# Three tiles ahead on ScalarE, one one-hot instruction for four tokens, and another order of fetches in a fused two-block kernel

## The reference, cut to what matters

```python
def peer_ffn(x, w_q, sub_keys, expert_u, expert_v):
    ...
    vals, ci = lax.top_k(cand, P_TOPK)
    e = (jnp.take_along_axis(i1, ci // P_TOPK, axis=-1) * N_KEYS
         + jnp.take_along_axis(i2, ci % P_TOPK, axis=-1))
    g = jax.nn.softmax(vals, axis=-1)
    ...
        a = jnp.einsum('cd,ckd->ck', xc, expert_u[ec])
        w = (gc * jax.nn.gelu(a.astype(jnp.float32))).astype(x.dtype)
        return jnp.einsum('ck,ckd->cd', w, expert_v[ec])
```

## Time and profile before

| | us |
|---|---|
| median of 3 runs (2543.43 to 2550.14) | 2543.64 |
| the profiled execution's own time | 2543.99 |
| its span, first to last instruction | 2542.3 |

### The profile page before, as it was taken

One profiled execution on the slowest core, in us unless ns is written; L12 is line 12 of the kernel. 1 busy time (PEld: TensorE's weight loads), 2 busy tenths in 40 slices (PEclk: granted clock), 3 DMA queues, 4 the chain that ended last, 5 costly groups with the idle time before them and its releaser, 6 DMA issues.

```text
span 2542.3 us, 39573 instructions
## 1 busy us (share of the span) xinstructions
PE 2397.2 (94%) x14819; PEld 2116.5 (83%) x14819; DVE 1463.5 (58%) x3355; ACT 1115.1 (44%) x1958; POOL 374.0 (15%) x338
## 2 busy tenths in 40 slices
PE   7999999999999888999999998888878999999999
PEld 4888788888785555779999998888877999999999
DVE  4444444333654485441899998777758773444443
ACT  4444343222442376343433448877853332332322
POOL 0000000000200000100001002222334313433330
PEclk9999999999998799998999999999998999999999
DMA  4223222322430000121556658887899988999992
GB/s 151 99 74 100 90 97 77 100 88 87 163 107 21 1 1 1 50 100 67 160 160 188 203 167 290 292 282 274 286 335 357 340 285 327 347 362 332 357 352 102
DMA packets 131823, 462.11 MB, mean 182 GB/s; under 512 B 13840, under 2 KB 32528, under 8 KB 129888
## 3 DMA queue, kind: packets, MB, share of 16 engines
q1 hardware_dynamic: 75744, 233.87, 26.9%
q0 software_dynamic: 51440, 196.90, 21.5%
q10 hardware_dynamic: 4496, 29.36, 3.0%
HBM read 407.12 MB, written 52.43 MB: 181 GB/s over the span
## 4 chain that ended last, share of the span: by engine, by line
PE 77%; DVE 12%; ACT 8%; DMA 1%; issue 1%; POOL 0%; ACTq 0%; SPq 0%; DVEq 0%; POOLq 0%
PE bank L427 13%; PE bank L428 13%; PE bank L429 13%; PE bank L1092 7%; PE bank L1093 7%; PE bank L1094 7%; DVE wlo L414 3%; PE bank L1105 2%; ACT stage L1478 2%; PE bank L442 2%; ACT hot L1464 1%; PE bank L1060 1%; PE bank L524 1%; ACT hot L1459 1%; ACT whi L410 1%; PE bank L707 1%
## 5 line engine op out<-in xcount | busy, mean ns | idle before, releaser
L414 DVE TENSOR_TENSOR wlo<-raw,whi 128x1024 fp32r<-128x1024 f32 x398 | 485.5, 1225 | 540.0 <-ACT whi L410 482.3
L427 PE MATMUL bank<-act_hi,whi 128*128 128x384 f32 (+1 forms) x1968 | 730.4, 371 | 31.9 <-DVE wlo L414 18.4
L428 PE MATMUL bank<-act_lo,whi 128*128 128x384 f32 (+1 forms) x1968 | 718.8, 365 | 0.0
L429 PE MATMUL bank<-act_hi,wlo 128*128 128x384 f32 (+1 forms) x1968 | 718.0, 365 | 0.0
L410 ACT ACTIVATE whi<-raw 128x1024 fp32r<-128x1024 f32 x398 | 418.3, 1056 | 288.2 <-PE bank L1094 175.2
L427 PEld LDWEIGHTS bank<-act_hi,whi 128*128 128x128 f32 x1968 | 375.8, 191 | 81.5 <-DVE wlo L414 21.0
L429 PEld LDWEIGHTS bank<-act_hi,wlo 128*128 128x128 f32 x1968 | 375.5, 191 | 38.1
L428 PEld LDWEIGHTS bank<-act_lo,whi 128*128 128x128 f32 x1968 | 376.0, 191 | 35.7 <-issue 0.5
L1092 PE MATMUL bank<-h_hi,whi 128*128 128x384 f32 x1024 | 350.2, 342 | 6.5 <-DVE h_lo L2196 6.5
L1093 PE MATMUL bank<-h_lo,whi 128*128 128x384 f32 x1024 | 348.0, 340 | 0.0
L1094 PE MATMUL bank<-h_hi,wlo 128*128 128x384 f32 x1024 | 345.8, 338 | 0.0
(11 more groups left out here) (354 smaller groups left out, 2765.5 us busy)
## 6 DMA issues: line engine op xcount, KB each, us to landing
raw<-tiles SPq DMA_DIRECT2D x398, 512.0 KB
acts_dram<-gelu SPq DMA_DIRECT2D x128, 192.0 KB
gates_dram<-stage ACTq DMA_DIRECT2D x12, 2048.0 KB
wg<-gates_dram POOLq DMA_DIRECT2D x16, 1536.0 KB
hf<-acts_dram POOLq DMA_DIRECT2D x16, 1536.0 KB
bias<-alibi POOLq DMA_DIRECT2D x16, 256.0 KB, 3.0
w1s<-cmp_w POOLq DMA_DIRECT2D x1, 4096.0 KB, 13.8
res<-x_t ACTq DMA_DIRECT2D x4, 512.0 KB, 10.0
```

Of the source, the lines that this page charges most:

```text
L414: dve.tensor_tensor(wlo[:, j.slot, :], raw[:, j.slot, :], whi[:, j.slot, :].bitcast(F32), ALU.subtract).then_inc(lo_made, 1)
L427: pe.matmul(to, wh, x, start=(kc == 0), stop=False)
L428: pe.matmul(to, wh, xl, start=False, stop=False)
L429: last = pe.matmul(to, wl, x, start=False, stop=(kc == KC - 1))
```

## The change

`make_hi` runs three jobs ahead of the results in all of the first block's loops, in the gate phase, in the rest of U and in V (`make_lo` stays two ahead). The four "equals i1" one-hots of a group are one DVE instruction with broadcast operands. The copy into `stage` walks bank and stage in another order: before it read the bank straight through and wrote single words 128 bytes apart; now it writes runs of four words and reads one word from each of the four tokens in turn. The dots are spread anew: two in every gate step, one in each of the eight jobs after it, so 96, 8 and 24 in place of 80, 16 and 32. POOL loads gates and activations of group 0 first, then two rows, then those of group 1. The first accumulation of V takes three groups in place of four (`V_HEAD`), and the quads run over the jobs 32 to 118 in place of 40 to 118.

```diff
-DOTS_GATES = [2, 2, 1]
-DOTS_REST = 2
+HI_AHEAD = 3
+DOTS_GATES = 2
+DOTS_REST = 1
 DOTS_V = 1
-V_HEAD = 4
+V_HEAD = 3
 V_WEIGHTS = GJ * V_HEAD + 1
-QUADS = {40 + r * 78 // 31: r for r in range(32)}
-SEEN_GATES = sum(DOTS_GATES) * 16
+QUADS = {32 + r * 86 // 31: r for r in range(32)}
+SEEN_GATES = DOTS_GATES * DT // 8
...
             load_gates(0)
-            load_gates(1)
             for m in range(RING):
                 pool.wait_ge(acts_stored[m], 16 * 5)
             load_acts(0)
+            for n in range(SEEN_GATES + ROWS, SEEN_GATES + ROWS + 2):
+                gather(n)
+            load_gates(1)
             load_acts(1)
+            for n in range(SEEN_GATES + ROWS + 2, SEEN_U + ROWS):
+                gather(n)
             pool.memset(spread[0][:, :], 0.0).then_inc(S("spread_zeroed"), 1)
-            for n in range(SEEN_GATES + ROWS, SEEN_U + ROWS):
-                gather(n)
...
-                make_hi(act, J(0).ahead())
-                make_hi(act, J(1).ahead())
+                make_hi(act, J(0).ahead(HI_AHEAD))
+                make_hi(act, J(1).ahead(HI_AHEAD))
...
-            def u_job(n):
+            def u_job(n, ahead=AHEAD):
                 j = Job(J_U + n)
-                make_hi(act, j.ahead())
+                make_hi(act, j.ahead(ahead))
                 activation_of(j, n // RING)
...
             weighted_hot(0)
+            make_hi(act, Job(J_U + U_GATES).ahead())
             for q in range(DT // 8):
-                u_job(U_GATES + q)
+                u_job(U_GATES + q, HI_AHEAD)
...
-                    act.activation(stage[:, buf, :, t:t + 4].rearrange("p j t -> p t j"),
-                                   bank[4 + gi % 4][:, :].rearrange("p (t j) -> p t j", t=4),
+                    act.activation(stage[:, buf, :, t:t + 4],
+                                   bank[4 + gi % 4][:, :].rearrange("p (t j) -> p j t", t=4),
                                    ACT.Copy).then_inc(S("gates_copied"), 1)
...
             for n in range(U_REST, P):
-                u_job(n)
+                u_job(n, HI_AHEAD)
...
-                    if not (last and dc + AHEAD >= KC):
-                        make_hi(act, Job(J_V + jj).ahead())
+                    if not (last and dc + HI_AHEAD >= KC):
+                        make_hi(act, Job(J_V + jj).ahead(HI_AHEAD))
...
-                    for x in range(4):
-                        t = 4 * gi + x
-                        ins = dve.tensor_scalar(hot[:, gi % 4 * 4 + x, 0, :], iota, selT[:, 0, t:t + 1], None, ALU.is_equal)
-                        if x < 2:
-                            dve.tensor_scalar(hot[:, gi % 4 * 4 + x, 1, :], iota, selT[:, 1, t:t + 1],
-                                              selT[:, 2, t:t + 1], ALU.is_equal, ALU.mult)
-                    ins.then_inc(S("hot_made"), 1)
-                for _ in range(DOTS_GATES[q % 3]):
+                    t, slot = 4 * gi, gi % 4 * 4
+                    for x in range(2):
+                        dve.tensor_scalar(hot[:, slot + x, 1, :], iota, selT[:, 1, t + x:t + x + 1],
+                                          selT[:, 2, t + x:t + x + 1], ALU.is_equal, ALU.mult)
+                    dve.tensor_tensor(hot[:, slot:slot + 4, 0, :], iota.unsqueeze(1).broadcast_to((P, 4, P)),
+                                      selT[:, 0, t:t + 4].unsqueeze(2).broadcast_to((P, 4, P)),
+                                      ALU.is_equal).then_inc(S("hot_made"), 1)
+                for _ in range(DOTS_GATES):
                     dot(seen)
```

More of the change, by code:

```diff
@@ L1132, in _ @@
                 act.activation(sq[:, kc, :], res[:, kc, :], ACT.Square).then_inc(sq_made, 1)
-            for m in range(AHEAD):
+            for m in range(HI_AHEAD):
                 make_hi(act, Job(m))
@@ L1168, in J @@
                     return Job(m, c, 8)
-                make_hi(act, J(0).ahead())
-                make_hi(act, J(1).ahead())
+                make_hi(act, J(0).ahead(HI_AHEAD))
+                make_hi(act, J(1).ahead(HI_AHEAD))
                 result_of(act, J(0))
                 act.activation(qT[:, :], bank[0][:, :], ACT.Copy).then_inc(taken[0], 1)
-                make_hi(act, J(2).ahead())
+                make_hi(act, J(2).ahead(HI_AHEAD))
                 result_of(act, J(1))
                 act.activation(kT[:, :], bank[1][:, :], ACT.Copy).then_inc(taken[1], 1)
-                make_hi(act, J(3).ahead())
+                make_hi(act, J(3).ahead(HI_AHEAD))
                 result_of(act, J(2))
                 act.activation(vT[:, :], bank[2][:, :], ACT.Copy).then_inc(taken[2], 1)
-                make_hi(act, J(4).ahead())
+                make_hi(act, J(4).ahead(HI_AHEAD))
                 result_of(act, J(3))
@@ L1185, in _ @@
                 exps(c, 0)
-                make_hi(act, J(5).ahead())
+                make_hi(act, J(5).ahead(HI_AHEAD))
                 exps(c, 1)
-                make_hi(act, J(6).ahead())
+                make_hi(act, J(6).ahead(HI_AHEAD))
                 copy_turned(c, 0)
-                make_hi(act, J(7).ahead())
+                make_hi(act, J(7).ahead(HI_AHEAD))
                 result_of(act, J(6))
@@ L1205, in _ @@
                 for h in range(2):
-                    make_hi(act, J(4 * h).ahead())
-                    make_hi(act, J(4 * h + 1).ahead())
+                    make_hi(act, J(4 * h).ahead(HI_AHEAD))
+                    make_hi(act, J(4 * h + 1).ahead(HI_AHEAD))
                     result_of(act, J(4 * h))
@@ L1210, in _ @@
                                    bias=half_b[:, bass.ds(i * 2 + h, 1)]).then_inc(taken[0], 1)
-                    make_hi(act, J(4 * h + 2).ahead())
-                    make_hi(act, J(4 * h + 3).ahead())
+                    make_hi(act, J(4 * h + 2).ahead(HI_AHEAD))
+                    make_hi(act, J(4 * h + 3).ahead(HI_AHEAD))
                     result_of(act, J(4 * h + 2))
@@ L1220, in _ @@
             for m in range(8):
-                make_hi(act, Job(J_C + m).ahead())
+                make_hi(act, Job(J_C + m).ahead(HI_AHEAD))
                 was_taken(act, Job(J_C + m))
@@ L1226, in _ @@
                 act.activation(sq2[:, m, :], hg[:, m, :], ACT.Square).then_inc(sq_made, 1)
-            make_hi(act, Job(J_D).ahead())
             make_hi(act, Job(J_D + 1).ahead())
```

## The result

The changed kernel takes **2461.01 us** (median of 4 runs, 2460.09 to 2464.21); the kernel before took 2546.16 us beside it (4 runs, 2543.43 to 2550.14; the 2543.64 of the forecast is the median of three of them). The ratio is 0.9667, 95% interval 0.9648 to 0.9685. Forecast were 2458, 2450 to 2482. The profiled execution took 2460.09 us.

The account below looks back on a forecast made before the run. PE, DVE and ACT taking turns in the gate phase (62 us) and late loads ahead of V (24 us) were taken as the bound; 2543.64 less 86 gives 2457.6, rounded to 2458 us, range 2450 to 2482.

Parts of the forecast that it names:

- The gate step: Gate phase: step falls from 7.37 to 6.05 us, PE's 5.97 plus 0.08, saving 62 us over 47 steps.
- the prediction's sign: Gate phase: as a sign of being right, DVE was to show no wait for `whi`, before 79.1 us.
- One-hots: Gate phase: the one DVE instruction of 512 columns that replaces four was to take 0.68 us.
- DVE's step: Gate phase: DVE's list with two dots was to need 5.67 us a step, below PE's 5.97.
- The copy: Gate phase: ACT's copy into `stage` was to take 0.8 us, between 600 ns and 1132 ns.
- "The slowest engine sets the step": Gate phase: the longest list, PE's 5.97 us, was to set the step, with 0.08 added for imperfect interlocking.
- The rival that ACT sets the step: Gate phase: with a slow strided read ACT needs 6.1 to 6.2 us a step, 2461 to 2465 us; 13 in 100.
- The transition: Gate phase's end through first V job: 64.8 us falls to 40.8, 24 us less, with PE's `h_lo` wait 2.2.
- The moved wait: V's start: late group 0 loads or row 106 make PE stand 5 to 20 us, 2463 to 2480; 10 in 100.
- Row 106: V's third job: row comes some 10 us late behind group 1's loads, covered with little to spare.
- The DMA rival: Gate phase: DMA engines set the step at 6.5 us, time 2478 to 2480 us; 14 in 100.
- First block and V: First block: 0, with 2 us either way; V: 0, as the later `h_lo` still lies under PE.

Follow-up runs that it names:

- old_hots: Changed kernel with the old one-hots, six instructions a group, taken back; 2463.74 us, ratio 0.9669.
- old_copy: Changed kernel with the old walk of the copy into `stage` taken back; 2466.58 us, ratio 0.9688.
- ahead_only: Kernel before the change with only ACT three jobs ahead from the gate phase on; 2481.19 us, ratio 0.9746.
- old_dots_split: Changed kernel with dots spread 80, 16 and 32 as before, but POOL's new order of loads; 2477.24 us, ratio 0.9726.
- acts_early: Changed kernel with group 0's activations loaded after the last gate product, ahead of the wait for the gate store; 2455.11 us, ratio 0.9639.
- first_two traces: Traces of two runs of the changed kernel with the first block's loops two tiles ahead again; medians 2455.57 and 2460.31 us.
- first_two_acts_early: Changed kernel with the first block two tiles ahead and group 0's activations loaded ahead of the gate store's wait; 2456.36 us, ratio 0.9645.
- acts_early_woven: Changed kernel with group 0's activations loaded early and each `weigh_lo` two places behind its `weigh`; 2454.99 us, ratio 0.9655.
- the four traces of the table above: Two traces of the changed kernel and two with its first block two tiles ahead; medians 2461.01, 2459.77, 2455.57 and 2460.31 us.
- first_two_again: Second run of the changed kernel with the first block two tiles ahead; 2460.31 us, ratio 0.9659, beside 2459.77 us for the changed kernel.

## Why the prediction was right

The total was 3 us off. The mechanism is that of the prediction in both places, but that the total is so close is partly luck: the gate phase gave 4.5 us more than forecast and the transition 6.1 us less.

- **The gate step**: forecast 6.05 us, measured 5.95, so 66.5 us in place of 62. I had added 0.08 because "three lists will not interlock perfectly". They did: no wait of PE for one-hots is left. DVE still waits for `whi` in some steps (11.8 us in all), against the prediction's sign, but within what it has to spare.
- **One-hots**: 0.68 us forecast, 0.681 measured. DVE's step is 5.67 as forecast: `make_lo` starts at 1699.13, and the list of one step, two groups of one-hots and two dots included, is through at 1704.80 (the last L2180 starts at 1704.19 and costs 0.61). In old_hots DVE's list sets the step, as its sum of 6.01 says.
- **The copy**: I took 0.8 us between 0.60 and 1.13; it is 0.579, the lower bound. By the Trainium skill ("SBUF — State Buffer", "Door 1: The DMA port swizzle") every read would have opened a new PSUM line and the copy stayed near 1.13; the row disagrees. What the section says of slow non-contiguous access to PSUM it says of matmuls, and the prediction carried it over to ACT. ACT's step is 5.1 us (5.3 forecast).
- **"The slowest engine sets the step"** is the rule of the sum that holds only in part. In old_copy and ahead_only ACT's list is the longest by 0.07 us, and PE does not feel it for 36 steps, because a lead of a tile is used up first; PE's own mean step is 5.97. The rival that ACT sets the step had 6.1 to 6.2, too much for the step. Its cost in time was not too high, since the late last store is paid ahead of V: old_copy takes 2.5 us more by the traces and 5.6 by the medians.
- **The transition**: forecast -24, measured -17.9. From the phase's end (1802.59, where job 120 starts) to V's first job done it is 46.9 us in place of 40.8. The eight jobs take 33.5 (33.0 forecast), the wait for `h_lo` is 6.82 in place of 2.2, and V's first job 6.51 in place of 4.12; 1.5 us of this was in reserve. Mis-sized is the landing of the loads: I put their issue 12.9 us after the phase's end, as before. It comes at +17.4, and the activations land at +35.9 in place of +31. In old_dots_split, where POOL has sixteen rows fewer to fetch in the phase, the issue comes at +11.4, and its wait for the store ends at 1813.1:

```profile
L675 POOLq EVENT_SEMAPHORE  x1: 17/17/17, 1813.1 to 1813.1; - x1
```

  So the new spread of the dots moves the issue by 6 us. The store lands 13.2 us after its issue in place of 9.5, which is 3.7 of them; the other 2.3 lie between the end of POOL's wait and its issue, 3.3 us in place of 1.0. That the store is slower for the rows in the DMA queues is the likely reading, and it fits the kernel before and ahead_only, which also have sixteen rows fewer and need 11.5 and 11.6 us from the issue of the store to that of the load, where the changed kernel needs 16.5. No run changes the rows alone. Once the activations are there early, as in acts_early, the wait is 1.74 us, near the 2.2 that gelu, `weigh_hi` and `weigh_lo` were to take.
- **The moved wait**, a rival (10 in 100), came about at the lower end of its 5 to 20 us: 6.8 us and the lower clock. The gate phase's surplus hid it in the total.
- **Row 106** waits 2.15 us, not 10, and is covered. The rest of U has no wait for a row; old_dots_split shows why.
- **The DMA rival** fell: the phase moved 377 GB/s at a share of 0.99 and no engine waited for a row or tile. The packets did not stay as slow as they were. Over 288 us that is also above the 358 GB/s of the Trainium skill ("DMA: Bandwidth & Descriptors", "Specifications"). Another page of the Trainium skill, "Perfetto Trace Analysis", section "Roofline", says that a core that is active alone can pull more than that share, and the trace agrees.
- **First block and V**: 0 and 0, as forecast.

What stays open is why POOL needs 3.3 us from the landed store to its issue in the changed kernel and 1.0 in old_dots_split, and what a smaller or earlier store would give; no kernel here has one. Nor is it settled why both first_two traces have the loads issued 1.6 to 3.2 us sooner than both traces of the changed kernel. first_two_acts_early, with +17.3, is sooner than acts_early and acts_early_woven too (+20.1 and +19.3); old_hots, with the first block three ahead, has +17.2. That the changed kernel has such executions is suggested by its fastest run of 2457.51: with 937.1 us from gate to end and the earliest gate phase seen here, it would take 1520.4 + 937.1 + 1.7 = 2459.2.

## What to carry to other kernels

Where three engines take turns, first give the one that others wait for a tile more of lead: here the lead alone took the step from 7.37 to 6.03, the shorter lists alone to 6.62, and both to 5.95, which is all PE's own work. What an edit is worth depends on which others are in, so measure it from both sides. A list that is slightly too long costs nothing until its lead is used up, but what it lags at the phase's end is paid where something waits for its last result. Behind a fixed store and load, issue first whatever does not depend on the store, and keep work that waits for a late row out of a queue that has urgent work behind it.

## What the runs showed of the hardware

- ACT copied a bank of 128 x 512 in 579 ns while reading words 512 bytes apart and writing runs of four. The straight copy was 600, and reading straight but writing single words 128 bytes apart 1126 to 1132 ns. Of these two walks only that of the write cost anything.
- One core moved 377 GB/s for 288 us at a DMA share of 0.99.
- In the four traces of the table above PE's wait of 2.96 to 7.00 us ahead of V was followed by 9 to 13 products at 1.2 GHz, and V's first job took 5.9 to 6.5 us. The length of the wait does not fix the price: 4.76 us cost 5.91 in first_two_again and 7.33 in old_hots. After waits of 1.74 us the job took 4.54 us at full clock in both kernels where DVE kept up.
- From the issue of the last 2 MB store to the issue of the load that waits for it 13.4 to 17.8 us passed in the kernels with 104 rows ahead of it, and 10.5 (1803.53 to 1814.04), 11.5 and 11.6 us in the three with 88. Executions of one kernel differ by 1.4 us in it, and over all kernels by up to 5.7 us in the stretch before the gate phase. To tell an effect of 5 us, run both kernels on one chip and look at the stage it is said to be in.
